# A two-block transformer layer on one core: dense expert weights made from 256-column products, modulation sums in two parts, and three pieces of reordering

## What is computed

```python
def second_block(x, c, w_ada, b_ada, ...):
    sc = jax.nn.silu(c)
    mod = sc @ w_ada[l] + b_ada[l]                    # 12288 columns: shifts, scales, gates
    sh1, sc1, ga1, sh2, sc2, ga2 = jnp.split(mod, N_ADA, axis=-1)
    h = _rmsnorm(x, g_mix[l]) * (1.0 + sc1) + sh1
    x = x + ga1 * _hybrid_mixer(h, ...)
    h = _rmsnorm(x, g_ffn[l]) * (1.0 + sc2) + sh2
    x = x + ga2 * _peer(h, peer_w_q, peer_k1, peer_k2, peer_u, peer_v)
    return _rmsnorm(x, g_final)

def _peer(h, w_q, k1, k2, u, vt):
    ...                                               # 16 of 16384 experts per token and head,
    w = jax.nn.softmax(vs, axis=-1)                   # from two lists of 128 keys
    act = jax.nn.gelu(jnp.einsum('thkd,td->thk', u[e], hx)) * wx
    return jnp.einsum('thk,thkd->td', act, vt[e])
```

## Time and profile before

| | |
|---|---|
| median of 3 runs | 3481.17 us (3480.73 to 3481.82) |
| the profiled execution | 3487.38 us, its span 3485.8 us |
| PE busy | 3426.2 us (98%) |
| PE weight loads busy | 2822.5 us (81%) |
| DVE busy | 2248.6 us (65%) |
| ACT busy | 1394.9 us (40%) |
| POOL busy | 482.1 us (14%) |
| DMA | 789.17 MB, 226 GB/s over the span |

### The profile page before, as it was taken

One profiled execution on the slowest core, in us unless ns is written; L12 is line 12 of the kernel. 1 busy time (PEld: TensorE's weight loads), 2 busy tenths in 40 slices (PEclk: granted clock), 3 DMA queues, 4 the chain that ended last, 5 costly groups with the idle time before them and its releaser, 6 DMA issues.

```text
span 3485.8 us, 41837 instructions
## 1 busy us (share of the span) xinstructions
PE 3426.2 (98%) x15760; PEld 2822.5 (81%) x15760; DVE 2248.6 (65%) x2053; ACT 1394.9 (40%) x1077; POOL 482.1 (14%) x293
## 2 busy tenths in 40 slices
PE   8999999999999999999998999999999999999998
PEld 7888888877887888778887888888888888888886
DVE  6664546787887887754575493445666655555556
ACT  6343434343333333443554344443333333333333
POOL 0000005200000000100000187663000000000000
PEclk9999999999999999999999999999999999999999
DMA  7555556788888888744454456767566565555552
GB/s 264 193 190 181 190 190 253 296 309 307 316 309 295 305 313 305 249 149 165 157 204 167 167 212 219 237 236 269 220 229 228 196 225 205 198 199 204 200 198 108
DMA packets 148934, 789.17 MB, mean 226 GB/s; under 512 B 14316, under 2 KB 47356, under 8 KB 61656
## 3 DMA queue, kind: packets, MB, share of 16 engines
q1 hardware_dynamic: 85680, 610.47, 48.1%
q0 software_dynamic: 25840, 145.80, 11.4%
q10 hardware_dynamic: 37312, 31.46, 2.8%
HBM read 751.96 MB, written 35.71 MB: 226 GB/s over the span
## 4 chain that ended last, share of the span: by engine, by line
PE 89%; DVE 4%; issue 2%; ACT 2%; DMA 1%; DVEq 0%; ACTq 0%; SPq 0%; POOLq 0%
PE ps L1757 28%; PE ps L1759 27%; PE ps L1758 27%; PE ps L1785 2%; PE ps L2252 2%; ACT hi L531 1%; DVE adaacc L1265 1%; DMA adaraw<-in_w_ada 1%; PE ps L1951 1%; DVE lo L999 1%; DVE y L1680 0%; PE ps L1887 0%; PE ps L1864 0%; PE ps L2073 0%; PE ps L1875 0%
## 5 line engine op out<-in xcount | busy, mean ns | idle before, releaser
L531 ACT CAST hi<-raw 128x2048 fp32r<-128x2048 f32 x576 | 1099.7, 1910 | 1857.0 <-PE ps L1759 1842.4
L999 DVE TENSOR_TENSOR lo<-raw,hi 128x2048 fp32r<-128x2048 f32 x500 | 1145.0, 2291 | 870.8 <-ACT hi L531 857.3
L1757 PE MATMUL ps<-hi,hTh 128*128 128x512 f32 x3040 | 1203.0, 396 | 0.7 <-DVE hTl L1007 0.7
L1759 PE MATMUL ps<-hi,hTl 128*128 128x512 f32 x3040 | 1186.2, 390 | 0.0
L1758 PE MATMUL ps<-lo,hTh 128*128 128x512 f32 x3040 | 1185.3, 390 | 0.0
L1757 PEld LDWEIGHTS ps<-hi,hTh 128*128 128x128 f32 x3040 | 572.5, 188 | 125.5 <-issue 9.5
L1759 PEld LDWEIGHTS ps<-hi,hTl 128*128 128x128 f32 x3040 | 571.8, 188 | 120.4
L1758 PEld LDWEIGHTS ps<-lo,hTh 128*128 128x128 f32 x3040 | 572.8, 188 | 114.3
L1757 PE MATMUL ps<-hi,pactTh 128*128 128x512 f32 x992 | 389.6, 393 | 2.8 <-DVE y L1680 2.6
L390 POOL TENSOR_TENSOR lo<-raw,hi 128x2048 fp32r<-128x2048 f32 x76 | 360.1, 4744 | 224.8 <-ACT hi L531 224.8
L1759 PE MATMUL ps<-hi,pactTl 128*128 128x512 f32 x992 | 386.5, 390 | 0.0
(11 more groups left out here) (349 smaller groups left out, 2288.1 us busy)
## 6 DMA issues: line engine op xcount, KB each, us to landing
raw<-in_w_peer SPq DMA_DIRECT2D x256, 1024.0 KB, 4.8
raw<-in_w_ffn SPq DMA_DIRECT2D x132, 1024.0 KB, 6.6
adaraw<-in_w_ada POOLq DMA_DIRECT2D x96, 1024.0 KB, 7.1
raw<-in_w_first SPq DMA_DIRECT2D x88, 1024.0 KB, 4.8
raw<-in_w_second SPq DMA_DIRECT2D x72, 1024.0 KB, 4.8
raw<-in_w_merge SPq DMA_DIRECT2D x28, 1024.0 KB, 5.0
w_scratch<-wst ACTq DMA_DIRECT2D x32, 512.0 KB, 3.3
wc<-w_scratch POOLq DMA_DIRECT2D x32, 512.0 KB, 4.7
```

Source lines behind the costliest of these rows:

```text
L531: nc.scalar.copy(hi[:, s, :], raw[:, s, :]).then_inc(hi_done, 1)
L999: V.tensor_tensor(lo[:, s, :], raw[:, s, :], hi[:, s, :].bitcast(F32), ALU.subtract).then_inc(lo_done, 1)
L1757: T.matmul(out, th[stat], hi[:, s, cut], start=start, stop=False)
L1759: return T.matmul(out, tl[stat], hi[:, s, cut], start=False, stop=stop)
```

## The change

The dense weights and the modulation sums get float32r operands in two parts, leading part and rest, with 256 and 512 columns a matmul. A batch of dense weights is four tokens in place of eight: four matmuls of 256 columns, where the moving operand holds the second keys times the weights' leading parts beside the same times their rests; ACT copies the leading half out, DVE adds the other (`weights_sum`), and there are 64 batches, behind the pieces of 16 early groups (8 to 23) in place of 8. So `EARLY` is 25: 24 down groups and 7 mixed groups take the place of 16 and 15; the number of pieces stays. For the modulation, ACT splits `adaacc` (`ada_hi`), DVE takes the rest (`ada_lo`), and four single-pass matmuls stand for the two of float32. The exponentials move one group ahead, POOL issues the first two loads of hidden values before the last rests, and in the down groups the sums into `y` stand ahead of the rests.

```diff
-W_GROUPS = SEQ // 32
+W_GROUPS = SEQ // 16
 EARLY = EARLY_TOP + W_GROUPS + 1
@@ gpsimd
+            pool.wait_ge(sem("hid_st"), 16 * 2)
+            pool.wait_ge(sem("one_hots"), 1)
+            load_hidden(0, 0)
+            load_hidden(1, 1)
+            for s in range(4):
+                rest_piece(Q_PEER + EARLY - 1, s)
             for u in range(2):
-                pool.wait_ge(sem(f"w_st{u}"), 16 * (SEQ // 16))
+                pool.wait_ge(sem(f"w_st{u}"), 16 * (SEQ // 8))
+            load_group(0, 0, hidden=False)
+            load_group(1, 1, hidden=False)
             pool.wait_ge(sem("hid_st"), 16 * (EARLY - 1))
-            load_group(0, 0)
-            load_group(1, 1)
@@ scalar
+            def ada_hi(a, u):
+                act.wait_ge(sem("ada_sum"), 16 * a + 16)
+                if not isinstance(a, int) or a >= 1:
+                    act.wait_ge(sem("ada_mm"), a)
+                nc.scalar.copy(adah[:], adaacc[:, u]).then_inc(sem("ada_hi"), 1)
...
                 round_piece(q + 1, s)
+                if j == 0:
+                    ada_hi(0, 0)
                 if j == 3:
                     silu(0)
+            ada_hi(1, 1)
...
                     gate_up_down(b, j)
+                    if j == 8:
+                        ada_hi(b + 2, u)
...
             def choice_exp(s):
-                if s == 0:
+                if s == 2:
...
-            early_group(EARLY_TOP - 2, 0, lambda s: None)
-            early_group(EARLY_TOP - 1, 1, choice_exp)
+            early_group(EARLY_TOP - 2, 0, choice_exp)
+            early_group(EARLY_TOP - 1, 1, lambda s: None)
...
+            def weights_out(n, v):
+                act.wait_ge(sem("weights_mm"), n + 1)
+                if not isinstance(n, int) or n >= 2:
+                    act.wait_ge(sem(f"w_st{v}"), 8 * (n - v))
+                nc.scalar.copy(wst[:, v], weight_parts[:, :, 0]).then_inc(sem("weights_out"), 1)
+            def store_weights(n, v):
+                act.wait_ge(sem("w_sum"), n + 1)
...
+            def weights_by(n, v):
+                weights_out(n, v)
+                if not isinstance(n, int) or n >= 1:
+                    store_weights(n - 1, 1 - v)
...
+            store_weights(SEQ // 4 - 1, 1)
@@ vector
+            def ada_lo(a, u):
+                dve.wait_ge(sem("ada_hi"), a + 1)
+                V.tensor_tensor(adal[:, u], adaacc[:, u], adah[:].bitcast(F32), ALU.subtract).then_inc(sem("ada_lo"), 1)
...
                 rest_piece(q + 1, s)
-                if j == 1:
+                if j == 0:
+                    ada_lo(0, 0)
+                if j == 2:
                     ada_row(0, 6)
                 ada_piece(1, j, 1, False)
             ffn_mul(0)
+            ada_lo(1, 1)
...
+                    if j == 9:
+                        ada_lo(b + 2, u)
...
+            def one_hots(n, v):
+                if not isinstance(n, int) or n >= 2:
+                    dve.wait_ge(sem("weights_mm"), n - 1)
...
+                V.tensor_tensor(oh2[:, v, :, 0], row, second, ALU.is_equal)
+                V.tensor_tensor(oh1[:, v], row, first, ALU.is_equal).then_inc(sem("one_hots_raw"), 1)
+                dve.wait_ge(sem("one_hots_raw"), n + 1)
+                chosen = oh2[:, v, :, 0].bitcast(F32)
+                V.tensor_tensor(oh2[:, v, :, 1], chosen, rest, ALU.mult).then_inc(sem("one_hots_lo"), 1)
+                dve.wait_ge(sem("one_hots_lo"), n + 1)
+                V.tensor_tensor(oh2[:, v, :, 0], chosen, weight, ALU.mult).then_inc(sem("one_hots"), 1)
+
+            def weights_sum(n, v):
+                dve.wait_ge(sem("weights_out"), n + 1)
+                V.tensor_tensor(wst[:, v], wst[:, v], weight_parts[:, :, 1], ALU.add).then_inc(sem("w_sum"), 1)
...
+            with dve.Fori(1, SEQ // 8) as i:
                 for v in range(2):
-                    one_hots(i, v, False)
+                    one_hots(2 * i + v, v)
+                    weights_sum(2 * i + (v - 1), 1 - v)
+            weights_sum(SEQ // 4 - 1, 1)
...
             def down_group(b, u, m):
                 for j in range(4):
+                    peer_down(b, j, 4 * b + (4 * (Q_PEER + EARLY) + j + 1))
                     if j == 2:
                         peer_lo(b + 1, 1 - u)
                     rest_piece(b + (Q_PEER + EARLY + 1), j)
-                    peer_down(b, j, 4 * b + (4 * (Q_PEER + EARLY) + j + 1))
@@ tensor
             def ada_sum(a, b, u):
-                pe.wait_ge(sem("ada_sum"), 16 * a + 16)
+                pe.wait_ge(sem("ada_lo"), a + 1)
...
-                    ins = T.matmul(ps[0:1, b + k, :], ones[:, 0:1], adaacc[:, u, 512 * k:512 * k + 512],
-                                   start=True, stop=True)
+                    half = slice(512 * k, 512 * k + 512)
+                    T.matmul(ps[0:1, b + k, :], onesr[:], adah[:, half], start=True, stop=False)
+                    ins = T.matmul(ps[0:1, b + k, :], onesr[:], adal[:, u, half], start=False, stop=True)
...
-                if s == 1:
+                if s == 2:
                     pe.wait_ge(sem("fold_t"), FOLD_FFN + 3)
                     ada_sum(0, 6, 0)
...
                 if not isinstance(n, int) or n >= 1:
-                    pe.wait_ge(sem("weights_out"), n)
-                for k in range(8):
-                    ins = T.matmul(ps[:, 4 + k // 4, P * (k % 4):P * (k % 4) + P], oh[:, v, 0, k],
-                                   oh[:, v, 1, k], start=True, stop=True)
+                    pe.wait_ge(sem("w_sum"), n)
+                for k in range(4):
+                    ins = T.matmul(ps[:, 4 + k // 2, SEQ * (k % 2):SEQ * (k % 2) + SEQ], oh1[:, v, k],
+                                   oh2[:, v, k].rearrange("p e b -> p (e b)"), start=True, stop=True)
```

More of the change, by code:

```diff
@@ L123 @@
     "ada_sum": "DVE: column tiles added up", "ada_used": "DVE: pieces used", "ada_mm": "PE: sums over partitions",
+    "ada_hi": "ACT: splits' leading parts", "ada_lo": "DVE: and rests", "onesr_in": "DVE: column of ones",
     "bada_in": "DMA: bias of a split", "modrow": "DVE: halves of a split", "mod_st": "DMA: splits in DRAM",
@@ L150 @@
     "picks_tr": "PE: turned", "one_hots_raw": "DVE: one-hot rows",
-    "one_hots": "DVE: and weighted", "weights_mm": "PE: eight tokens' dense weights", "weights_out": "ACT: out of PSUM",
+    "one_hots_lo": "DVE: times the weights' rests", "one_hots": "DVE: and times their leading parts",
+    "weights_mm": "PE: four tokens' dense weights, both parts", "weights_out": "ACT: leading parts out of PSUM",
+    "w_sum": "DVE: rests added to them",
     "w_st0": "DMA: even batches in DRAM", "w_st1": "DMA: odd batches in DRAM",
```

83 lines of the change are left out of this document (42 added, 41 removed).

## The result

The changed kernel takes **3440.74 us** (median of 4 runs, 3440.50 to 3443.16) against 3481.18 us of the kernel before on the same chip: ratio 0.9885, 95% interval 0.9868 to 0.9902. That is 40.4 us faster. 3433.3 was predicted, with 3427 to 3447 as the range.

The account below looks back on a forecast made before the run. PE, busy 3426.2 of 3485.8 us, was taken as the bound. Savings of 28.2 (dense weights), 9.6 (modulation), 1.8 (choice) and 8.3 (down groups) sum to 47.9 us: 3481.2 becomes 3433.3, range 3427 to 3447.

Parts of the forecast that it names:

- Dense weights: Early stage: 32 batches of 1.80 us become 64 of 0.46 us on PE, saving 28.2 us.
- I take 0.46 with its handover: Dense weights: price of a batch of four 256-column matmuls, each 0.112 to 0.117 us, 0.45 to 0.47 in all.
- Rival 2: Dense weights: weight loads bound the 256-column matmuls, 0.76 us a batch, saving 9.0 instead of 28.2, 3452 us; chance 0.05.
- rival 3: Early stage: the loop around `w_sum` or POOL's rests becomes a wait of 0.1 to 0.3 us a batch, 3440 to 3452; chance 0.05.
- Down groups: Sums into `y` taken before the rests remove a 0.56 us stall in 16 groups; 8.3 us saved (6 to 9).
- rival 5: Down groups keep their 0.56 us because the wait comes from the piece's end: 3441, or 3446 us; chance 0.05.
- End of the early stage: From the last early piece to the first down product: weights land about 15 us after, wanted at 15.7; 0 taken, 0 to 2 at risk.
- Modulation: Feed-forward part: single-pass sums save 10.8 us nominally, 9.6 us after corrections at the start (8.4 to 11).
- 0.90 saved: Modulation: each sum falls from 1.81 to 0.91 us as four single-pass matmuls; twelve sums give 10.8 us.
- the loss at the start: Feed-forward's start: first split's 0.9 us lost, DVE 1.2 us later, 0.9 us regained from the half-clock sum.
- Rival 4: Feed-forward part turns DVE-bound as ACT waits in `ada_hi`; in all ten groups the 9.6 us are gone, 3443 us; chance 0.08.
- I take the same saving off the median: Sum: the 47.9 us worked out against the profiled 3487.38 us is subtracted from the median 3481.17 us, 6.2 us lower.

Follow-up runs that it names:

- experiment 6: Changed kernel with each batch's four 256-column weight products made twice, the second over the first: 3467.16 us, ratio 0.9957.
- experiment 7: Changed kernel with every 256-column weight product cut into two of 128 columns, same type and data: 3466.66 us, ratio 0.9957.
- experiment 10: Changed kernel with the first group's product before the last modulation steps, DVE's modulation steps spread over twelve pieces, sums behind the fifth piece: 3431.18 us, ratio 0.9853.
- experiment 1: The kernel before, unchanged, run and profiled again: 3481.8 us median, ratio 1.0; its profiled execution took 3481.5 us.
- experiment 5: The changed kernel, unchanged, run and profiled again: 3439.59 us, ratio 0.9878.
- experiments 8 and 9: Changed kernel with the feed-forward's start reordered and PE's sums one piece later (8: 3441.44 us), or the same with sums behind the sixth piece (9: 3442.25 us).
- experiment 4: Kernel before with the dense weights' part and POOL's moved loads; modulation, exponentials and order of sums into `y` as before: 3465.45 us, ratio 0.9944.
- experiment 11: Kernel with spread modulation steps, but DVE's first-group product put back behind its last two modulation steps: 3437.87 us, ratio 0.987.
- experiment 8: Changed kernel with DVE's first-group product before the last modulation steps, ACT's leading part later, PE's sums one piece later: 3441.44 us, ratio 0.9885.

## Why the prediction was right, and where it was off

**Direction and size** were right: PE's work that went away is what went from the time, and no other engine took its place.

**Dense weights**, 28.2 forecast, 25.6 measured: 32 x 1.80 - 64 x 0.50. The mis-sized step is "I take 0.46 with its handover": on the chain four products take 0.47, but by the spacing of the batches 0.50, and in experiment 6 four more cost 0.48, 0.12 each. The reasoning that a record of 128 columns and one of 256 cost the same was right, and experiment 7 shows it in the same type: between 128 and 256 columns it is the number of products with a full load of their own that counts, halved from 512 records to 256. Rival 2, one bare load after another, is out: four loads of 0.19 us, 0.76 in all, stand in a batch of 0.47.

The Trainium skill ("TensorE: Matmul & The Clock Gate", Part 3, "The mechanism") says that a weight load overlaps with running matmuls only when the row groups differ; the same section names a background weight buffer as a second way for a load to run ahead. These runs do not agree with the rule in its strict form: full loads of 0.19 us belong to products that are 0.12 us apart.

**The early stage's cover**, against rival 3: right. POOL's rests took 4.63 us, DVE's sum ended 2.6 us before PE asked (2.0 forecast), and experiment 6 shows that the stage follows PE alone.

**Down groups**, 8.3 forecast: 36.0 - 25.6 - 1.9 = 8.5 measured; rival 5 is out. **Choice**, 1.8 forecast, 1.9 measured. **End of the early stage**, 0 taken, 0 to 2 at risk: 0 in one execution, 1.9 in another, and up to 3.5 in the variants, 5.2 with the half clock behind the wait (experiment 10).

**Modulation**, 9.6 forecast, 9.3 and 10.4 by medians. By stages it is 11.0: the feed-forward part took 757.8 to 761.2 us in the four profiles with the old sums (mean 759.6) and 745.9 to 750.9 in the six with the new sums in the changed kernel's order (mean 748.6). The number was right for partly wrong reasons, since two terms were mis-sized and nearly cancel.

The first is "0.90 saved" a sum. A steady group, from one turn of `fact` to the next, went from 68.2 to 67.1 us, so a sum saves 1.1 and twelve save 13.2, where 10.8 were forecast. Of the 1.1, 0.88 lie in the sum itself (1.81 to 0.93); the rest lies at its edges, where the float32 matmuls stood 0.32 us behind the piece before them, and the second matmul of the next piece 0.34 us behind its first, in place of 0.23 (profile of experiment 1).

The second is the loss at the start, 1.2 us net by the forecast (0.9 for the first split and 1.2 for DVE, less 0.9 for the half clock). The forecast saw that DVE sets PE's time there and foresaw 3 to 6 us of waiting for `fact` and `factTl` with some half clock (4.9 came). But the 0.9 us that it gained back at half clock came from the first profile, and three other profiles with the old sums have no half clock there. PE's waits in the feed-forward part were 3.3 to 7.2 us with the old sums (mean 4.9) and 4.5 to 7.6 with the new (mean 6.3), and every profile in the changed kernel's order has some 1.6 us or more of half clock besides. So the start lost some 3 us and not 1.2, and 13.2 - 3 is about 10. Rival 4 came true in the first group alone: in experiment 5 all full groups behind it are 67.1 us long.

**The step that failed** is "I take the same saving off the median". The profiled execution of before was 6.2 us above the median, and that excess was taken as belonging to profiled executions. It was not: the next profiled execution took 3481.5 us, right at the median. That 46.6 us lie between the two first profiles, close to the 47.9 of the sum, is in part luck: from the second profile of before to the first of the changed kernel it is 40.7. Only 40.4 or 42.9 us came off the median, and 42.3 when all 60 timed runs of before (median 3482.75) and the eight of the changed kernel (3440.4) are taken together.

2.3 us of the difference to 47.9 are the dense weights, the down groups and the choice together (36.0 for 38.3), and up to 2.1 are the end of the early stage, taken as 0. From the keys to the end the saving is thus 34 to 36 us, and with 11.0 for the feed-forward the stages give 45 to 47, some 3 to 5 us above the 42.3 of whole runs. Some 1.7 of that is that the two profiled executions of before average 3484.4 us, above their median. The rest is no more than single profiles of one kernel differ by, and stays open.

## What to carry to other kernels

Where PE bounds and products are narrow, count products with their weight loads, not columns: doubling the columns of a float32r product from 128 to 256 was free here (0.119 and 0.12 us), while 512 cost 0.227, so merging two narrow results into one wider product is what pays. An engine that is 66% busy over the kernel can still be behind for 50 us of it; then moving the wait only renames it (experiments 8 and 9), and what helps is to spread the work that caused the backlog over the place where the engine has slack (experiment 10). Before a saving is worked out from a wait in one profile, take a second profile of the same kernel: what differs between the two is no term. And take the price of a piece of work from the spacing of what stands around it, not from its own rows: the float32 sums cost 0.2 us more than their own 1.81.

## What was not expected of the hardware

- A float32r product of 128 columns with a load of its own took 0.105 us on the chain and, with what it costs its neighbours, 0.95/8 = 0.119; one of 256 columns 0.12; one of 512 columns 0.227.
- After a wait of 3.7 us PE ran at the lower level (1.2 GHz) until 782.98, which cost some 1.6 us more; in all these profiles each wait of PE for DVE of 2.9 us or more in the feed-forward part or for `pact` had the half clock behind it. Of the shorter ones that of 2.1 us in experiment 4 had it too, while those of 2.5 us in experiment 11 and 2.7 us for `pact` in experiment 8 did not.
- The changed kernel showed feed-forward parts of 749.6 and 745.9 us, and waits of 0.2 and 2.1 us for `pact`, with nothing changed.
